# Residual GEMMs: the high weights stream high and low input as one matmul of 512 columns, and VectorE adds up two halves of a bank

## The chip, the cores and the metric

The kernel runs on one core of a Trainium2 chip. The metric is the device time of one execution in microseconds (us). A change of some 0.2% (3 us) is at the edge of what can be measured here.

## The reference

Two blocks of two layers each work on one sequence of T = 256 tokens and a width D = 1024. All matrix products are asked for in fp32:

```
block 1, layer 0: z = S5 mixer with GLU;        h = LN(a*h + z @ w_out);  h = LN(a*h + (silu(h@Wg) * (h@Wu)) @ Wdown)
block 1, layer 1: o = stick-breaking attention; h = LN(a*h + o @ w_o);    h = LN(a*h + SwiGLU(h) @ Wdown)
block 2, twice:   m = gated mix of windowed attention and mLSTM
                  x = x + m @ w_out;   u = relu(rmsnorm(x) @ w_ff1);   x = x + (u*u) @ w_ff2
```

with a = 4^(1/4). The eight products that are added to the running state (here called residual GEMMs) are the ones that the change is about: their depth is 1024 for the four w_out kinds, 2816 for the two Wdown, 4096 for the two w_ff2, and each gives 1024 x 256 results.

## The kernel before

**Split products.** Every fp32 matrix product is made of three in the type fp32r: each operand is split into a high part (a copy rounded to fp32r) and a low part (the rest), and high x high + high x low + low x high are summed in PSUM. The helper `three` (L399 to L402) issues them: `w_hi` with the input's high part, `w_hi` with its low part, `w_lo` with its high part. Each of the three is a load of 128x128 weights and a matmul of 256 columns (the tokens).

**Chunks.** Weights are streamed in chunks of 128x2048 (16 blocks of 128x128, 1 MB) through a ring of three buffers (`RING`): SyncE's DMAs bring `raw` (L371), ScalarE copies it to `w_hi` (`split_hi`, L376) once the chunk that had the buffer is used up (`chunk_done`), VectorE subtracts to get `w_lo` (`split_lo`, L381), and TensorE (PE) waits for that. The order on each engine is written out by hand, in `resid_tensor`, `resid_scalar` and `resid_vector` and their kin.

**Residual GEMMs** in the order of the program: ssm_out (0), down0 (1), sb_out (2), down1 (3), out0 (5), ff2_0 (6), out1 (7), ff2_1 (8). Their input lies in `hid_hi` and `hid_lo` (each 32 blocks of 256 tokens). The result is cut into KT = 8 tiles of 128 features x 256 tokens; a tile sums 8, 22 or 32 blocks in the first half (256 fp32) of a PSUM bank, three banks in turn (`tile_bank`). Of the ssm_out kind (shape kt8) the first chunk makes tiles 0 and 1 together, waiting for the hid blocks one by one (`resid_first`), and `resid_blocks` does the rest; of the others (shape col) `resid_blocks` does everything, tile by tile. A tile beyond the third waits until VectorE has emptied its bank (`resid_done`).

**What VectorE does with a tile.** `add_tile` (L633) adds it to `res`, scaled; before a layer norm (n < 4) tiles 4 to 7 go by `shifted_tile` (L957) to `xn`, whose mean over four tiles has been taken off ahead of time (`shift_sum` on VectorE, L939 and L941; `shift_mean` on PE, L705; `shifted_tiles`, L947 and L949). Between the tiles VectorE has the w_lo splits and, for the next GEMM, `raw_lo` or `x_lo` (L980, L998), and the sums of squares (L987, L989), while ScalarE has the w_hi splits, `raw_hi` or `x_hi` (L809, L793) and the squares (L769, L779); both take these in a fixed order. After the last tile PE makes the first chunks of the next GEMM from the not yet normed values (`early_tensor`, 258 columns) and the sums of the norm (L712 to L727), VectorE turns them into the scale (from the copy L1004 on), and ScalarE and VectorE norm four pairs of tiles in turn before they split the next weights.

Of the kernel before, what the change touches and what calls it, by code (L numbers as in the profile page):

```python
# [16 lines left out]
F32R = mybir.dt.float32r  # L17
# [3 lines left out]
ALU = mybir.AluOpType  # L21
# [3 lines left out]
P = 128  # L25
T = 256
D = 1024
KT = D // P
# [214 lines left out]
def stack(nc, w, out):  # L243
# [4 lines left out]
    with ctx:  # L248
# [14 lines left out]
        def sb(name, shape, region, off=0, dt=F32):  # L263
            return nc.alloc_sbuf_tensor_at(name, shape, dt, offset=place[region] + off)
# [5 lines left out]
        res = sb("res", [P, KT, T], "res")  # L270
        x_hi = sb("x_hi", [P, KT, T], "xh", 0, F32R)
        x_lo = sb("x_lo", [P, KT, T], "xl", 0, F32R)
        hid_hi = sb("hid_hi", [P, 32, T], "hh", 0, F32R)
        hid_lo = sb("hid_lo", [P, 32, T], "hl", 0, F32R)
        xn = sb("xn", [P, KT, T], "xc")
        sqr = sb("sqr", [P, 2, 512], "sq")
        gate_sb = sb("gate_sb", [P, RING, 512], "sg")
# [118 lines left out]
        def tile_bank(g, t):  # L396
            return OUT_BANKS[t % 3] if g.half else (g.bank0 + t) % 3

        def three(dst, lhs_hi, lhs_lo, r_hi, r_lo, start, stop):  # L399
            nc.tensor.matmul(dst, lhs_hi, r_hi, start=start, stop=False, skip_group_check=True)  # L400
            nc.tensor.matmul(dst, lhs_hi, r_lo, start=False, stop=False, skip_group_check=True)  # L401
            return nc.tensor.matmul(dst, lhs_lo, r_hi, start=False, stop=stop, skip_group_check=True)  # L402

        def weights_split(pe, chunk):
            pe.wait_ge(lo_done, chunk + 1)

# [81 lines left out]
        def resid_first(pe, g, kts=(0, KT)):  # L488

            if kts[0] == 0:  # L490
                weights_split(pe, g.c0)
                if g.half:
                    pe.wait_ge(hid_done, g.in_hid + 2)
                elif g.before.evac == "gated":
                    pe.wait_ge(z_done, g.before.gated0 + g.before.n - 1)
            s = g.c0 % RING
            hi, lo = kt8_view(w_hi, s), kt8_view(w_lo, s)
            t0 = 8 if g.half else 0
            for kt in range(*kts):
                pe.wait_ge(hid_done, g.in_hid + (kt // 2 if g.half else kt) + 1)  # L500
                for m in range(2):
                    last = three(PS[:, tile_bank(g, m), 0:T], hi[:, kt, m, :], lo[:, kt, m, :], hid_hi[:, t0 + kt, :],
                                 hid_lo[:, t0 + kt, :], kt == 0, kt == KT - 1)
                    if kt == KT - 1:
                        last.then_inc(chunk_done if m else tile_done, 1)

        def resid_blocks(pe, g, idx, j0=0, j1=16):
# [5 lines left out]
            for j in range(j0, j1):  # L513
# [11 lines left out]
                    hi, lo = kt8_view(w_hi, s)[:, kt, j // KT, :], kt8_view(w_lo, s)[:, kt, j // KT, :]  # L525
                else:
                    hi, lo = w_hi[s][:, cols], w_lo[s][:, cols]
                last = three(PS[:, tile_bank(g, t), 0:T], hi, lo, hid_hi[:, t0 + kt, :], hid_lo[:, t0 + kt, :], kt == 0,
                             kt == g.kts - 1)
                if j == 15:  # L530
                    last.then_inc(chunk_done, 1)
                elif kt == g.kts - 1:
# [96 lines left out]
        def add_tile(dve, g, t):  # L629
            tile_ready(dve, g, t)  # L630
            if t == 0 and g.normed:
                dve.wait_ge(res_normed, g.normed)
            nc.vector.scalar_tensor_tensor(out=res[:, t, :], in0=res[:, t, :], scalar=g.alpha, in1=PS[:, tile_bank(g, t), 0:T],  # L633
                                           op0=ALU.mult, op1=ALU.add).then_inc(resid_done, 1)

        def mix_bank(half, which, q):
            return (4 + half + 2 * q) if which == 0 else 2 * half + q
# [316 lines left out]
        def shifted_tile(dve, g, n, t):  # L954

            tile_ready(dve, g, t)
            nc.vector.tensor_tensor(xn[:, t, :], xn[:, t, :], PS[:, tile_bank(g, t), 0:T], ALU.add).then_inc(resid_done, 1)  # L957
            if t >= 5:
                dve.wait_ge(resid_done, g.resid0 + t + 1)

# [1728 lines left out]
```

## Time and profile before

| | |
|---|---|
| median of 3 executions | 1462.29 us (1461.01 to 1462.5) |
| the profiled execution | 1462.21 us, of which the span from first to last instruction is 1460.4 us |
| mean granted clock of TensorE | 0.98 |
| PE busy | 1383.9 us, 95%, 11695 matmuls |
| VectorE busy | 958.0 us, 66% |
| ScalarE busy | 689.7 us, 47% |
| DMA | 227.54 MB, mean 156 GB/s, queue 1 busy 54.2% of 16 engines |
| chain that ended last | PE 72%, VectorE 12%, ScalarE 9% |

PE is TensorE's matmuls, PEld its weight loads, DVE VectorE, ACT ScalarE. A matmul's duration runs from its start to its modelled end, and the next one starts before that, so a pace is read from starts. In brackets behind a row stands how long the engine had been idle before it, and who released it. Lines are those of the kernel before.

### The profile page before, as it was taken

To read this page: it belongs to the slowest core of one execution; us is meant where nothing else is said; L and a number is where in the kernel's file an instruction comes from. 1 tells how busy PE (TensorE), PEld (TensorE's weight loads), DVE (VectorE), ACT (ScalarE), POOL (GpSimd) and SP (SyncE) were. 2 spreads that over 40 slices of the span, in tenths; PEclk is the share of its full clock that TensorE was granted. 3 is DMA by queue.
4 is the path that set the end of the run, shared out by engine and by line. 5 is a ranking of instruction groups with operands and counts; after the bars stand their busy time and mean duration, and the time that the engine had idled before them with its cause. 6 is when DMAs were issued, how large, how long until landed. Compare 5 with 4: busy or idle time off the path is not lost.

```text
span 1460.4 us, 27765 instructions
## 1 busy us (share of the span) xinstructions
PE 1383.9 (95%) x11695; PEld 1342.4 (92%) x11695; DVE 958.0 (66%) x1255; ACT 689.7 (47%) x853; POOL 10.1 (1%) x8
## 2 busy tenths in 40 slices
PE   5759999999999999999989999999999999999998
PEld 4548999999988899999979998999999999899998
DVE  7996687555664587555787567765447756777542
ACT  4746463343565363343556454444344644444432
POOL 0100000000000000000000000000000000000000
PEclk7779999999999999999999999999999999999999
DMA  5078557676452457666444354557665435465761
GB/s 127 1 109 218 177 142 202 181 191 175 145 171 90 116 143 203 176 190 182 145 145 121 111 173 153 194 176 198 174 182 165 125 107 174 145 200 173 195 180 58
DMA packets 340448, 227.54 MB, mean 156 GB/s; under 512 B 21672, under 2 KB 335248, under 8 KB 340128
## 3 DMA queue, kind: packets, MB, share of 16 engines
q1 hardware_dynamic: 340352, 226.14, 54.2%
q8 instruction: 75, 1.23, 0.4%
q14 instruction: 21, 0.17, 0.0%
HBM read 222.70 MB, written 1.05 MB: 153 GB/s over the span
## 4 chain that ended last, share of the span: by engine, by line
PE 72%; DVE 12%; ACT 9%; issue 3%; SPq 2%; DMA 1%; ACTq 0%; DVEq 0%
PE PS L400 22%; PE PS L402 21%; PE PS L401 21%; DVE w_lo L381 5%; ACT w_hi L376 4%; SPq L1430 1%; PE PS L1163 1%; ACT res L815 1%; PE PS L1482 1%; DMA x_chunk<-in_x_dram 1%; PE PS L1498 1%; DVE raw_lo L980 1%; DVE sqr L987 1%; ACT x_group L1595 0%; PE PS L1463 0%
## 5 line engine op out<-in xcount | busy, mean ns | idle before, releaser
L381 DVE TENSOR_TENSOR w_lo<-raw,w_hi 128x2048 fp32r<-128x2048 f32 x208 | 475.8, 2291 | 210.0 <-ACT w_hi L376 209.9
L400 PE MATMUL PS<-x_hi,w_hi 128*128 128x256 f32 x1824 | 522.2, 286 | 8.1 <-DVE w_lo L381 7.0
L401 PE MATMUL PS<-x_lo,w_hi 128*128 128x256 f32 x1824 | 517.2, 284 | 0.0
L402 PE MATMUL PS<-x_hi,w_lo 128*128 128x256 f32 x1824 | 517.1, 283 | 0.0
L376 ACT ACTIVATE w_hi<-raw 128x2048 fp32r<-128x2048 f32 x208 | 397.1, 1910 | 230.6 <-PE PS L402 227.8
L400 PEld LDWEIGHTS PS<-x_hi,w_hi 128*128 128x128 f32 x1824 | 350.9, 192 | 12.5 <-DVE w_lo L381 8.0
L400 PE MATMUL PS<-hid_hi,w_hi 128*128 128x256 f32 x1248 | 354.5, 284 | 6.6 <-DVE hid_lo L664 6.6
L401 PE MATMUL PS<-hid_lo,w_hi 128*128 128x256 f32 x1248 | 353.1, 283 | 0.0
L402 PE MATMUL PS<-hid_hi,w_lo 128*128 128x256 f32 x1248 | 353.1, 283 | 0.0
L401 PEld LDWEIGHTS PS<-x_lo,w_hi 128*128 128x128 f32 x1824 | 351.2, 193 | 0.1
L402 PEld LDWEIGHTS PS<-x_hi,w_lo 128*128 128x128 f32 x1824 | 350.9, 192 | 0.0
L400 PEld LDWEIGHTS PS<-hid_hi,w_hi 128*128 128x128 f32 x1248 | 239.5, 192 | 7.8 <-DVE hid_lo L664 7.4
L401 PEld LDWEIGHTS PS<-hid_lo,w_hi 128*128 128x128 f32 x1248 | 239.6, 192 | 0.1
L402 PEld LDWEIGHTS PS<-hid_hi,w_lo 128*128 128x128 f32 x1248 | 239.5, 192 | 0.0
L545 ACT ACTIVATE gate_sb<-PS 128x256 f32<-128x256 f32 x48 | 18.4, 383 | 147.8 <-PE PS L402 147.8
L548 ACT ACTIVATE gate_sb<-gate_sb 128x512 f32<-128x512 f32 x32 | 20.3, 633 | 99.3 <-DVE gate_sb L601 99.3
L588 DVE TENSOR_TENSOR prod<-PS,gate_sb 128x256 f32<-128x256 f32 x48 | 20.3, 424 | 64.5 <-ACT gate_sb L545 64.4
L633 DVE SCALAR_TENSOR_TENSOR res<-res,PS 128x256 f32<-128x256 f32 x48 | 19.9, 418 | 39.2 <-PE PS L402 39.0
L400 PE MATMUL PS<-w_hi,x_hi 128*128 128x256 f32 x128 | 37.5, 293 | 0.0
L400 PE MATMUL PS<-raw_hi,w_hi 128*128 128x258 f32 x128 | 36.9, 288 | 0.0
L998 DVE SCALAR_TENSOR_TENSOR x_lo<-res,vec,x_hi 128x256 fp32r<-128x256 f32 x32 | 15.2, 484 | 33.0 <-ACT x_hi L793 33.0
L401 PE MATMUL PS<-w_lo,x_hi 128*128 128x256 f32 x128 | 36.1, 282 | 0.0
(363 smaller groups left out, 1377.3 us busy)
## 6 DMA issues: line engine op xcount, KB each, us to landing
raw<-in_w_ff_dram SPq DMA_DIRECT2D x128, 512.0 KB, 4.5
raw<-in_ffn_w_gu_dram SPq DMA_DIRECT2D x88, 512.0 KB, 5.2
raw<-in_w_in_dram SPq DMA_DIRECT2D x68, 512.0 KB, 4.8
raw<-in_sb_w_qkv_dram SPq DMA_DIRECT2D x24, 512.0 KB, 4.5
raw<-in_ffn_w_down_dram SPq DMA_DIRECT2D x20, 512.0 KB, 4.6
raw<-in_ssm_w_glu_dram SPq DMA_DIRECT2D x16, 512.0 KB, 6.4
raw<-in_w_out_dram SPq DMA_DIRECT2D x16, 512.0 KB, 4.5
raw<-in_ssm_w_out_dram SPq DMA_DIRECT2D x8, 512.0 KB, 4.5
```

Source lines behind the costliest of these rows:

```text
L376: nc.scalar.activation(w_hi[s][:, :], raw[s][:, :], ACT.Copy).then_inc(hi_done, 1)
L381: nc.vector.tensor_tensor(w_lo[s][:, :], raw[s][:, :], w_hi[s][:, :].bitcast(F32), ALU.subtract).then_inc(lo_done, 1)
L400: nc.tensor.matmul(dst, lhs_hi, r_hi, start=start, stop=False, skip_group_check=True)
L401: nc.tensor.matmul(dst, lhs_hi, r_lo, start=False, stop=False, skip_group_check=True)
L402: return nc.tensor.matmul(dst, lhs_lo, r_hi, start=False, stop=stop, skip_group_check=True)
L545: nc.scalar.activation(gate_sb[:, k, 0:T], PS[:, bank, T:2 * T], g.func).then_inc(sig_done, 1)
L548: nc.scalar.activation(gate_sb[:, k, :], gate_sb[:, k, :], ACT.Square).then_inc(u_done, 1)
L588: nc.vector.tensor_tensor(prod[:, 0:T], PS[:, bank, 0:T], gate_sb[:, k, 0:T], ALU.mult).then_inc(z_done, 1)
L633: nc.vector.scalar_tensor_tensor(out=res[:, t, :], in0=res[:, t, :], scalar=g.alpha, in1=PS[:, tile_bank(g, t), 0:T], op0=ALU.mult, op1=AL ...
L815: nc.scalar.activation(res[:, kt, :], xn[:, kt, :], ACT.Identity, scale=gain(n, kt), bias=ln_bias(n, kt)).then_inc(res_normed, 1)
L980: nc.vector.scalar_tensor_tensor(out=raw_lo[:, t, 0:T], in0=xn[:, t, :], scalar=raw_gain(n, t), in1=raw_hi[:, t, 0:T].bitcast(F32), op0=AL ...
L998: nc.vector.scalar_tensor_tensor(out=x_lo[:, t, :], in0=res[:, t, :], scalar=gain(n, t), in1=x_hi[:, t, :].bitcast(F32), op0=ALU.mult, op1 ...
```

## The change

`hid_hi` and `hid_lo` become the two halves of one tensor, `hid_both`, at the same addresses. The new helper `halves` takes the place of `three` in the residual GEMMs, for tiles 0 to 6: one matmul of `w_hi` with the high and low input as 512 columns (2 x 256, from two places 32 KB apart in each partition) into both halves of the bank, and one of `w_lo` with the high input, 256 columns, into the first half. Tile 7 keeps `three`. VectorE adds the second half of the bank to `res` or `xn` with an operation of its own: in `add_tile` after the first one, in `shifted_tile` before it, and the second of the two waits for the first (`dve_step`). The mix and all other GEMMs stay with `three`.

```diff
--- before.py
+++ after.py
@@ -270,8 +270,8 @@
         res = sb("res", [P, KT, T], "res")
         x_hi = sb("x_hi", [P, KT, T], "xh", 0, F32R)
         x_lo = sb("x_lo", [P, KT, T], "xl", 0, F32R)
-        hid_hi = sb("hid_hi", [P, 32, T], "hh", 0, F32R)
-        hid_lo = sb("hid_lo", [P, 32, T], "hl", 0, F32R)
+        hid_both = sb("hid_both", [P, 2, 32, T], "hh", 0, F32R)
+        hid_hi, hid_lo = hid_both[:, 0, :, :], hid_both[:, 1, :, :]
         xn = sb("xn", [P, KT, T], "xc")
         sqr = sb("sqr", [P, 2, 512], "sq")
         gate_sb = sb("gate_sb", [P, RING, 512], "sg")
@@ -400,6 +400,15 @@
             nc.tensor.matmul(dst, lhs_hi, r_hi, start=start, stop=False, skip_group_check=True)
             nc.tensor.matmul(dst, lhs_hi, r_lo, start=False, stop=False, skip_group_check=True)
             return nc.tensor.matmul(dst, lhs_lo, r_hi, start=False, stop=stop, skip_group_check=True)
+
+        def halves(bank, lhs_hi, lhs_lo, both, start, stop):
+
+            nc.tensor.matmul(PS[:, bank, :].rearrange("p (a t) -> p a t", a=2), lhs_hi, both, start=start, stop=False,
+                             skip_group_check=True)
+            return nc.tensor.matmul(PS[:, bank, 0:T], lhs_lo, both[:, 0, :], start=False, stop=stop, skip_group_check=True)
+
+        def in_halves(t):
+            return t < KT - 1
 
         def weights_split(pe, chunk):
             pe.wait_ge(lo_done, chunk + 1)
@@ -499,8 +508,8 @@
             for kt in range(*kts):
                 pe.wait_ge(hid_done, g.in_hid + (kt // 2 if g.half else kt) + 1)
                 for m in range(2):
-                    last = three(PS[:, tile_bank(g, m), 0:T], hi[:, kt, m, :], lo[:, kt, m, :], hid_hi[:, t0 + kt, :],
-                                 hid_lo[:, t0 + kt, :], kt == 0, kt == KT - 1)
+                    last = halves(tile_bank(g, m), hi[:, kt, m, :], lo[:, kt, m, :], hid_both[:, :, t0 + kt, :],
+                                  kt == 0, kt == KT - 1)
                     if kt == KT - 1:
                         last.then_inc(chunk_done if m else tile_done, 1)
 
@@ -525,8 +534,11 @@
                     hi, lo = kt8_view(w_hi, s)[:, kt, j // KT, :], kt8_view(w_lo, s)[:, kt, j // KT, :]
                 else:
                     hi, lo = w_hi[s][:, cols], w_lo[s][:, cols]
-                last = three(PS[:, tile_bank(g, t), 0:T], hi, lo, hid_hi[:, t0 + kt, :], hid_lo[:, t0 + kt, :], kt == 0,
-                             kt == g.kts - 1)
+                if in_halves(t):
+                    last = halves(tile_bank(g, t), hi, lo, hid_both[:, :, t0 + kt, :], kt == 0, kt == g.kts - 1)
+                else:
+                    last = three(PS[:, tile_bank(g, t), 0:T], hi, lo, hid_hi[:, t0 + kt, :], hid_lo[:, t0 + kt, :], kt == 0,
+                                 kt == g.kts - 1)
                 if j == 15:
                     last.then_inc(chunk_done, 1)
                 elif kt == g.kts - 1:
@@ -630,8 +642,15 @@
             tile_ready(dve, g, t)
             if t == 0 and g.normed:
                 dve.wait_ge(res_normed, g.normed)
-            nc.vector.scalar_tensor_tensor(out=res[:, t, :], in0=res[:, t, :], scalar=g.alpha, in1=PS[:, tile_bank(g, t), 0:T],
-                                           op0=ALU.mult, op1=ALU.add).then_inc(resid_done, 1)
+            bank = tile_bank(g, t)
+            first = nc.vector.scalar_tensor_tensor(out=res[:, t, :], in0=res[:, t, :], scalar=g.alpha, in1=PS[:, bank, 0:T],
+                                                   op0=ALU.mult, op1=ALU.add)
+            if not in_halves(t):
+                first.then_inc(resid_done, 1)
+                return
+            first.then_inc(dve_step, 1)
+            dve.wait_ge(dve_step, v_count.one())
+            nc.vector.tensor_tensor(res[:, t, :], res[:, t, :], PS[:, bank, T:2 * T], ALU.add).then_inc(resid_done, 1)
 
         def mix_bank(half, which, q):
             return (4 + half + 2 * q) if which == 0 else 2 * half + q
@@ -954,7 +973,11 @@
         def shifted_tile(dve, g, n, t):
 
             tile_ready(dve, g, t)
-            nc.vector.tensor_tensor(xn[:, t, :], xn[:, t, :], PS[:, tile_bank(g, t), 0:T], ALU.add).then_inc(resid_done, 1)
+            bank = tile_bank(g, t)
+            if in_halves(t):
+                nc.vector.tensor_tensor(xn[:, t, :], xn[:, t, :], PS[:, bank, T:2 * T], ALU.add).then_inc(dve_step, 1)
+                dve.wait_ge(dve_step, v_count.one())
+            nc.vector.tensor_tensor(xn[:, t, :], xn[:, t, :], PS[:, bank, 0:T], ALU.add).then_inc(resid_done, 1)
             if t >= 5:
                 dve.wait_ge(resid_done, g.resid0 + t + 1)
```

## Rows read from the trace of the kernel before

**Rows 1.** The page, busy us, share of the span, instructions.

```profile
PE 1383.9 (95%) x11695; PEld 1342.4 (92%) x11695; DVE 958.0 (66%) x1255; ACT 689.7 (47%) x853; POOL 10.1 (1%) x8
```

**Rows 2.** The page, costliest groups: busy, mean ns of one, idle before, releaser.

```profile
L400 PE MATMUL PS<-hid_hi,w_hi 128*128 128x256 f32 x1248 | 354.5, 284 | 6.6 <-DVE hid_lo L664 6.6
```

**Rows 3.** Windows (length, busy of each engine, clock, DMA share, GB/s), ff2 of layer 0.

```profile
995.50:1088.00 92.50, 92.50 (x773) 92.50 (x772) 46.15 (x38) 37.42 (x30) 0.00 (x0) 1.00 0.65 183
```

**Rows 4.** Timeline of PE (start, duration, us), ff2 of layer 0, first and last.

```profile
995.54 0.28 PE L400 MATMUL PS<-hid_hi,w_hi 128*128 128x256 f32 x1
...
1087.58 0.28 PE L402 MATMUL PS<-hid_hi,w_lo 128*128 128x256 f32 x1
```

**Rows 5.** Timeline of PE, 258-column matmuls without a wait, first and last of 54.

```profile
193.61 0.28 PE L401 MATMUL PS<-raw_lo,w_hi 128*128 128x258 f32 x1
...
199.95 0.28 PE L400 MATMUL PS<-raw_hi,w_hi 128*128 128x258 f32 x1
```

**Rows 6.** Windows and timeline of PE at granted clock 0.50, attention of block 2.

```profile
768.00:769.00 1.00, 1.00 (x6) 1.00 (x6) 0.50 (x3) 0.39 (x2) 0.00 (x0) 0.50 0.00 0
...
768.20 0.41 PE L400 MATMUL PS<-x_hi,w_hi 128*128 128x256 f32 x1
...
770.55 0.41 PE L402 MATMUL PS<-x_hi,w_lo 128*128 128x256 f32 x1
```

**Rows 7.** Timeline of PE, plain fp32 matmuls of the norm after ssm_out.

```profile
191.33 0.59 PE L725 MATMUL PS<-xn,const 128*128 128x256 f32 x2
...
193.06 0.59 PE L718 MATMUL PS<-sqr,const 128*128 128x256 f32 x2
```

**Rows 8.** Timeline of PE's weight loads behind the plain fp32 matmul in down0.

```profile
354.35 0.19 PEld L400 LDWEIGHTS PS<-hid_hi,w_hi 128*128 128x128 f32 x1
354.56 0.19 PEld L401 LDWEIGHTS PS<-hid_lo,w_hi 128*128 128x128 f32 x1
354.68 0.19 PEld L402 LDWEIGHTS PS<-hid_hi,w_lo 128*128 128x128 f32 x1
```

**Rows 9.** Timeline of PE, plain fp32 matmuls of 129 columns.

```profile
813.21 0.39 PE L2059 MATMUL PS<-vm_tok,m_w 128*128 128x129 f32 x2
813.43 0.39 PE L2060 MATMUL PS<-vm_tok,m_w 128*128 128x129 f32 x2
```

**Rows 10.** Timeline of VectorE, two operations of which one waits for the other.

```profile
194.62 0.42 DVE L1004 COPY dm_sb<-PS 128x256 f32<-128x256 f32 x1
195.07 0.42 DVE L1006 TENSOR_TENSOR rstd<-dm_sb,PS 128x256 f32<-128x256 f32 x1
```

**Rows 11.** Windows and timeline, the norm after ssm_out: VectorE's stretch, its start, PE's wait.

```profile
178.20:194.60 16.40, 16.40 (x128) 16.04 (x127) 16.07 (x23) 9.36 (x15) 0.00 (x0) 1.00 0.38 102
...
176.28 1.92 ACT L376 ACTIVATE w_hi<-raw 128x2048 fp32r<-128x2048 f32 x1 [2.22 <-PE PS L402]
...
209.66 0.39 PE L400 MATMUL PS<-x_hi,w_hi 128*128 128x256 f32 x1 [1.66 <-DVE w_lo L381]
```

**Rows 12.** Timeline, down0 and its norm: waits of PE, the chain's start and copy.

```profile
354.03 0.30 PEld L705 LDWEIGHTS PS<-prod,const 128*128 128x128 f32 x2 [0.29 <-DVE prod L941]
...
366.27 1.91 ACT L376 ACTIVATE w_hi<-raw 128x2048 fp32r<-128x2048 f32 x1 [1.20 <-PE PS L402]
...
389.41 0.42 DVE L1004 COPY dm_sb<-PS 128x256 f32<-128x256 f32 x1
...
404.23 0.39 PE L400 MATMUL PS<-x_hi,w_hi 128*128 128x256 f32 x1 [0.90 <-DVE w_lo L381]
```

**Rows 13.** Timeline, out0: PE behind the mix, tile 7's x_lo, PE behind the squares.

```profile
882.83 0.38 PE L400 MATMUL PS<-hid_hi,w_hi 128*128 128x256 f32 x1 [1.61 <-DVE hid_lo L664]
...
905.54 0.48 DVE L998 SCALAR_TENSOR_TENSOR x_lo<-res,vec,x_hi 128x256 fp32r<-128x256 f32 x1 [0.58 <-ACT x_hi L793]
...
908.19 0.70 PE L714 MATMUL PS<-sqr,const 128*128 128x256 f32 x2 [0.19 <-ACT sqr L779]
```

## The prediction

> **What bounds the kernel now.** I read the page's busy times first: TensorE is busy 95% of the span [rows 1], so the question is what its matmuls are paced by. The costliest groups show the operation that the change touches: 1248 triples on hid [rows 2], of which 128 belong to the mix GEMMs and 1120 to the residual ones (4 x 64 + 2 x 176 + 2 x 256). The windows show a long residual stage, ff2 of layer 0: PE is busy for all of it, VectorE for half, at clock 1.00 [rows 3]. The timeline gives the pace, which the mean duration of 283 ns hides because matmuls overlap: from the first to the last start of that stage are 767 steps in 92.04 us, 120.0 ns a step [rows 4]. Then I read, in the timelines of VectorE and ScalarE, the places where PE does wait: the layer norms at the end of ssm_out, down0, sb_out and down1, and the end of out0 and out1.
>
> **What a step of 120 ns consists of.** Four rows bound it. The 258-column matmuls take 53 steps in 6.34 us, 119.6 ns, no more than 256 columns do [rows 5]: neither a rate per column nor a fixed cost on top of the columns sets the 120 ns, or 258 would be slower by almost 1 ns. At granted clock 0.50 (1.2 GHz) the same fp32r matmuls take 11 steps in 2.35 us, 213.6 ns, which is 256/1.2 = 213.3 with nothing beside it [rows 6]. At full clock the plain fp32 matmuls of the norm, which also load 128x128, take 1.73 us for eight (four lines, x2 each), 216 ns [rows 7]. The weight loads behind such a matmul start at 354.35, 354.56 and 354.68: 0.21 after the long one, 0.12 after the short one, each load with the start of the matmul before its own [rows 8]. So I read: a load of fp32r weights starts when the matmul ahead starts and takes 120 ns; a matmul with less than that to stream waits for it, one of 213 ns hides it.
>
> **The pair in place of the triple.** One triple: 3 x 120 = 360 ns. New: 512 columns (512/2.4 = 213.3; 216 by rows 7) with the low load hidden, then 256 columns under which the next high load takes its 120: 336 ns. It saves 24 ns. Bounds: the most is 360 - 213 - 110 = 37 ns, if the short one went at the 110 ns that plain fp32 loads show (0.22 us for two) [rows 9]; the least is 360 - 512 x 0.464 - 120 = 2.5 ns, if 119.6/258 = 0.464 ns were a rate per column [rows 5]. I take 24, since rows 6 to 8 agree on it. Pairs: 980 (all residual triples but those of tile 7: 1120 - 140). 980 x 24 ns = 23.5 us off PE's own work. How much of it arrives is a matter of each stage.
>
> The Trainium skill (TensorE: Matmul & The Clock Gate, section Back-to-back issue gap) gives N/2.4 + 2.5 ns for a warm matmul, 109 ns at 256 columns. The trace disagrees with 120.0 [rows 4]. By that rule a pair would save one fixed 2.5 ns, 2.5 us in all: it speaks against this change, and its time is that of rival 2.
>
> **What VectorE pays.** Seven tiles of eight get a second add, behind a wait for the first one. A dependent 128x256 operation follows its forerunner after 0.45 us [rows 10]. 56 x 0.45 = 25 us more on VectorE, which has room in the ff2 stages [rows 3] and none in the norm tails. Its wait stands on VectorE's own semaphore, so everything behind it there slips by 0.45: the split into w_lo, raw_lo, the sums.
>
> *ff2_0 and ff2_1.* 224 pairs each, no wait of PE inside. Their last tile keeps the triple, so the end has one add as now. The loads stay hidden: a chunk goes from 5.76 to 5.38 us, DMA share 0.65 to 0.70 [rows 3], and ScalarE's 1.9 plus VectorE's 2.3 us a chunk are still under it. 2 x 224 x 24 ns = -10.8 us.
>
> *ssm_out and sb_out.* In the 16.4 us before the norm VectorE is busy 16.07, with no gap [rows 11]. The stretch begins when chunk 1 is done (ScalarE's w_hi at 176.28, VectorE's w_lo at 178.23) [rows 11] and ends with the copy at 194.62 [rows 10]; the norm's result lets PE go on at 209.66, after a wait of 1.66 [rows 11]. In ssm_out chunk 1 comes 32 x 24 ns = 0.77 earlier, but tile 3's second add (0.45) eats most of it: w_lo starts 0.45 earlier. Tiles 4, 5 and 6 add 3 x 0.45 = 1.35. Net +0.9. In sb_out the pairs before PE's wait for the last heads gain nothing, 24 remain (0.58), w_lo starts 0.27 earlier: net +1.1. The PE time saved there becomes a longer wait.
>
> *down0 and down1.* PE already waits 0.29 at the shift's matmul for VectorE's sum (the load at 354.03) [rows 12]. That sum comes from chunk 4 (80 pairs, -1.92) plus tile 3's 0.45, so at -1.47, though PE is there at -2.30: 0.83 is lost. Two chunks later (32 pairs, 0.77) chunk 7 is done at -2.24, and from there ScalarE's w_hi at 366.27 starts a chain through VectorE and ScalarE, in turn, to the copy at 389.41 and to PE's restart at 404.23 [rows 12]. It has the second adds of tiles 5 and 6, +0.90. Net -1.34 each, -2.7 for both.
>
> *out0 and out1.* The first block waits for VectorE's mix until 882.83 [rows 13], so 44 pairs remain, 1.06 us. But each tile goes ScalarE's x_hi, VectorE's x_lo, next add in turn. Tile 1's second add is absorbed by idle time ahead of tile 2's x_hi; those of tiles 3 and 4 (0.9) use up the idle time there and the 0.9 by which chunk 2 comes earlier, with +0.1 left at tile 4's x_hi; those of 5 and 6 come on top: +1.0 at tile 7's x_lo, now 905.54 [rows 13]. PE is early by 1.06 and waits for it. The squares follow, and there PE already waits 0.19 [rows 13]. Net +1.0 each, +2.0.
>
> Sum: -10.8 - 2.7 + 0.9 + 1.1 + 2.0 = -9.5. The profiled execution took 1462.2 us (span 1460.4 and 1.8 around it), the median is 1462.29; so **1452.7 us**.
>
> **Rivals.**
> (1) *VectorE's adds cost nothing on the path, and the PE time arrives whole*: -23.5, 1438.7 us. For it: PE at 95%. Against it: rows 11 to 13, where PE waits for that chain at the end of six stages. Chance 0.08.
> (2) *The change makes it slower because the 512 columns stream at a rate per column.* Place: the long matmul; price: 238 ns instead of 216. A pair then saves 2.5 ns, ff2 gives -1.1 in all, the downs about +1.0 each, ssm_out and sb_out +1.35 each, out0 and out1 +1.4 each: +6.4, 1468.6 us. It decides from a saving of some 10 ns a pair downward. The same holds if the input from two regions 32 KB apart is streamed as two pieces with the load repeated: the change then wouldn't do what it says. Against it: 258 columns take no longer than 256 [rows 5]. Chance 0.06. (The rule of the Trainium skill above would give a pair the same 2.5 ns.)
> (3) *The 13 ns over 106.7 are a fixed cost per matmul.* A pair saves 13.3 ns: ff2 -6.0, the downs -0.1 each, ssm_out and sb_out +1.3 each, out0 and out1 +1.2 each: -1.2, 1461.0 us. For it: 120 - 106.7 = 13.3 is there in every step. Against it: 216 rather than 227 [rows 7], and rows 5. Chance 0.12.
> The forecast's mechanism holds the remaining 0.74.
>
> **How the numbers follow.** The likeliest case gives 1452.7. Its own range is 1446 to 1459: a pair at 37 ns gives 1444 to 1446, and 15 ns with 0.6 us an add gives some 1460. The range to hold 8 of 10 is 1445 to 1461: it takes in most of case 3 and leaves out 1 and 2. A difference of 0.2% (2.9 us) is about what a measurement of this kernel can tell. Faster than 1459.4: the forecast, case 1 and little of case 3, 0.83. Within: most of case 3, 0.10. Slower: case 2 and a misjudged VectorE, 0.07.
>
> **What would show it.** 980 matmuls fewer. In ff2 the start of a long matmul to the next short one 0.21 to 0.22 (case 3: 0.227, case 2: 0.238), from there 0.12; the stage in 86.7 instead of 92.0 us. The copy of the norm later than now, counted from chunk 1, in ssm_out and sb_out, and PE's waits there at about 3.9 us in place of 1.66 (56 x 24 ns = 1.3 earlier, 0.9 later). At the shift of down0 a wait of 1.1 us. In out0, tile 7's x_lo later against the end of the mix by 1.0. The forecast is wrong if the short matmul doesn't keep to 120, if the second add follows after other than 0.45, or if the tails of the norms move with PE.

## The result: 0.4% slower, and the profile after

| | before | after |
|---|---|---|
| median, executions | 1462.50 us, 7 | 1468.77 us, 7 |
| ratio, 95% interval | | 1.0039, 1.0026 to 1.0051 |
| profiled execution, its span | 1462.2, 1460.4 | 1467.8, 1466.0 |

The forecast was 1452.7 us, 1445 to 1461. By the interval the change made the kernel slower by 3.8 to 7.5 us. One of the seven executions after took 1522 us, at a mean granted clock of 0.845 where the others have 0.974 to 0.991, and is not in the ratio.

The page of the kernel after, in the order of [rows 1, 2] (the lines of the file have shifted: L406 is the matmul of 512 columns, L408 the one of 256 behind it):

```profile
PE 1384.1 (94%) x10715; PEld 1294.0 (88%) x10715; DVE 979.3 (67%) x1311; ACT 689.6 (47%) x853; POOL 10.1 (1%) x8
...
L406 PE MATMUL PS<-hid_both,w_hi 128*128 128x512 f32 x980 | 348.3, 400 | 6.7 <-DVE hid_both L683 6.7
...
L408 PE MATMUL PS<-hid_both,w_lo 128*128 128x256 f32 x980 | 275.6, 281 | 0.0
```

There are 980 matmuls fewer (11695 - 10715) and 56 VectorE operations more, as counted; PE's busy time has not moved (1383.9 to 1384.1). The window over ff2 of layer 0 [rows 3] and PE's timeline in it, first, a few in the middle, last [rows 4]:

```profile
1004.45:1095.00 90.55, 90.55 (x546) 80.13 (x545) 48.89 (x44) 37.37 (x29) 0.00 (x0) 1.00 0.67 186
...
1004.45 0.40 PE L406 MATMUL PS<-hid_both,w_hi 128*128 128x512 f32 x1
...
1010.10 0.40 PE L406 MATMUL PS<-hid_both,w_hi 128*128 128x512 f32 x1
1010.34 0.28 PE L408 MATMUL PS<-hid_both,w_lo 128*128 128x256 f32 x1
1010.46 0.40 PE L406 MATMUL PS<-hid_both,w_hi 128*128 128x512 f32 x1
1010.69 0.28 PE L408 MATMUL PS<-hid_both,w_lo 128*128 128x256 f32 x1
...
1094.99 0.28 PE L402 MATMUL PS<-hid_both,w_lo 128*128 128x256 f32 x1
```

The stage takes 90.54 us from start to start, 1.50 less than before, where 5.4 was forecast. Tile 7's triples are 95 steps of 0.12 (11.4 us); the 224 pairs share the other 79.14: **353.3 ns a pair, 6.7 less than a triple**. From long to short are some 0.235, from short to long 0.118.

The ends of the other stages, [rows 11 to 13] after the change. PE's timeline first, then ScalarE and VectorE in the norm behind ssm_out (w_hi, w_lo, copy), in the one behind down0 (w_hi, copy) and at the end of out0 (tile 7's x_lo, PE behind the squares):

```profile
210.21 0.39 PE L400 MATMUL PS<-x_hi,w_hi 128*128 128x256 f32 x1 [1.76 <-DVE w_lo L381]
355.97 0.70 PE L724 MATMUL PS<-prod,const 128*128 128x256 f32 x2 [0.66 <-DVE prod L960]
406.85 0.39 PE L400 MATMUL PS<-x_hi,w_hi 128*128 128x256 f32 x1 [1.76 <-DVE w_lo L381]
543.17 0.39 PE L400 MATMUL PS<-x_hi,w_hi 128*128 128x256 f32 x1 [1.77 <-DVE w_lo L381]
739.09 0.39 PE L400 MATMUL PS<-x_hi,w_hi 128*128 128x256 f32 x1 [2.43 <-DVE w_lo L381]
...
175.29 1.92 ACT L376 ACTIVATE w_hi<-raw 128x2048 fp32r<-128x2048 f32 x1 [2.12 <-PE PS L408]
177.44 2.28 DVE L381 TENSOR_TENSOR w_lo<-raw,w_hi 128x2048 fp32r<-128x2048 f32 x1
195.19 0.42 DVE L1027 COPY dm_sb<-PS 128x256 f32<-128x256 f32 x1
...
368.00 1.93 ACT L376 ACTIVATE w_hi<-raw 128x2048 fp32r<-128x2048 f32 x1 [1.09 <-PE PS L408]
...
392.05 0.42 DVE L1027 COPY dm_sb<-PS 128x256 f32<-128x256 f32 x1
...
914.45 0.48 DVE L1021 SCALAR_TENSOR_TENSOR x_lo<-res,vec,x_hi 128x256 fp32r<-128x256 f32 x1 [0.58 <-ACT x_hi L812]
...
917.09 0.70 PE L733 MATMUL PS<-sqr,const 128*128 128x256 f32 x2 [0.22 <-ACT sqr L798]
```

Every wait at a norm has grown, those that end at 210.21 and 543.17 by 0.1 us only (before: 1.66, 0.90, 1.65 and 1.64 for the four in order; after: 1.76, 1.76, 1.77 and 2.43). Measured from the first matmul of a residual GEMM to PE's restart behind the norm (for out0 and out1 from the mix's end to the last squares), the stages moved so:

| us | ssm_out | down0 | sb_out | down1 | out0 | ff2_0 | out1 | ff2_1 | sum |
|---|---|---|---|---|---|---|---|---|---|
| before | 45.10 | 85.01 | 47.26 | 85.75 | 25.36 | 92.04 | 25.37 | 92.04 | |
| after | 46.43 | 85.62 | 48.66 | 86.36 | 26.54 | 90.54 | 26.55 | 90.55 | |
| moved | +1.33 | +0.61 | +1.40 | +0.61 | +1.18 | -1.50 | +1.18 | -1.49 | **+3.3** |

The medians moved by 6.3 and the ratio says 5.7, so 2.4 to 3 us are not in the stages. The windows show what else differs: two places right behind waits at a norm, in the kernel after and then at the same times before (length, busy time of each engine, clock, DMA share, GB/s).

```profile
210.00:215.00 5.00, 4.79 (x27) 4.79 (x28) 4.93 (x8) 0.51 (x1) 0.00 (x0) 0.66 0.74 199
740.00:743.00 3.00, 3.00 (x16) 3.00 (x15) 2.93 (x5) 0.63 (x1) 0.00 (x0) 0.50 0.94 288
```

```profile
210.00:215.00 5.00, 5.00 (x44) 5.00 (x43) 4.93 (x8) 0.65 (x2) 0.00 (x0) 1.00 0.86 228
740.00:743.00 3.00, 2.90 (x27) 1.81 (x26) 1.75 (x5) 2.46 (x8) 0.00 (x0) 1.00 0.75 237
```

After the waits that end at 210.21 and 739.09, PE runs 15 steps each at clock 0.50, every one 213 ns in place of 120. I call such a step slow; it costs 0.093 us. Past the first 125 us, PE's timeline has 27 slow steps before and 65 after: +3.5 us in this pair of profiles, of which 30 steps (2.8 us) stand behind those two waits; the other 35, and the 27 of before, lie in the attention of block 2 (765 to 830 and 1184 to 1190). With the stages' +3.3, and the stretch ahead of ssm_out, which happened to be 0.8 shorter (163.78 in place of 164.56), that makes 6.0 us; the two spans differ by 5.6.

### The profile page after: what moved, and what is told of

It reads as the page before. It is cut to its first block, busy times and chain, and to the rows that moved or that the text cites. A ratio compares the mean times of both kernels' runs of the same rounds, so it can differ in the third digit from the quotient of the medians.

```text
span 1466.0 us, 25861 instructions
## 1 busy us (share of the span) xinstructions
PE 1384.1 (94%) x10715; PEld 1294.0 (88%) x10715; DVE 979.3 (67%) x1311; ACT 689.6 (47%) x853; POOL 10.1 (1%) x8
## 4 chain that ended last, share of the span: by engine, by line
PE 70%; DVE 14%; ACT 9%; issue 3%; SPq 2%; DMA 1%; ACTq 0%; DVEq 0%
PE PS L400 15%; PE PS L401 15%; PE PS L402 15%; PE PS L406 12%; PE PS L408 6%; DVE w_lo L381 5%; ACT w_hi L376 4%; SPq L1453 1%; PE PS L1186 1%; DMA x_chunk<-in_x_dram 1%; PE PS L1505 1%; ACT x_hi L812 1%; ACT res L834 1%; DVE raw_lo L1003 1%; PE PS L1521 1%
## 5 line engine op out<-in xcount | busy, mean ns | idle before, releaser
L406 PE MATMUL PS<-hid_both,w_hi 128*128 128x512 f32 x980 | 348.3, 400 | 6.7 <-DVE hid_both L683 6.7
L402 PEld LDWEIGHTS PS<-x_hi,w_lo 128*128 128x128 f32 x1824 | 353.3, 194 | 0.0
L408 PE MATMUL PS<-hid_both,w_lo 128*128 128x256 f32 x980 | 275.6, 281 | 0.0
L406 PEld LDWEIGHTS PS<-hid_both,w_hi 128*128 128x128 f32 x980 | 184.4, 188 | 53.2 <-DVE hid_both L683 8.0
L408 PEld LDWEIGHTS PS<-hid_both,w_lo 128*128 128x128 f32 x980 | 185.6, 189 | 0.1
L402 PE MATMUL PS<-hid_both,w_lo 128*128 128x256 f32 x268 | 76.0, 284 | 0.0
L401 PE MATMUL PS<-hid_both,w_hi 128*128 128x256 f32 x268 | 76.0, 284 | 0.0
L400 PE MATMUL PS<-hid_both,w_hi 128*128 128x256 f32 x268 | 76.0, 283 | 0.0
L400 PEld LDWEIGHTS PS<-hid_both,w_hi 128*128 128x128 f32 x268 | 51.5, 192 | 0.4
L402 PEld LDWEIGHTS PS<-hid_both,w_lo 128*128 128x128 f32 x268 | 51.5, 192 | 0.0
L401 PEld LDWEIGHTS PS<-hid_both,w_hi 128*128 128x128 f32 x268 | 51.5, 192 | 0.0
```

Of the source, the lines that this page charges most:

```text
L406: nc.tensor.matmul(PS[:, bank, :].rearrange("p (a t) -> p a t", a=2), lhs_hi, both, start=start, stop=False, skip_group_check=True)
L408: return nc.tensor.matmul(PS[:, bank, 0:T], lhs_lo, both[:, 0, :], start=False, stop=stop, skip_group_check=True)
```

## Experiments

My theory after the comparison had three terms: a pair saves 6.7 ns and not 24 (why, was open); the second adds lengthen the ends of six stages as the prediction's account of VectorE has it; PE's longer waits bring on stretches at half clock. Twelve runs were made, of eleven kernels. "Before" was timed beside each set, at 1462.4 to 1463.5 us.

**1. Matmuls by themselves** (`bench`; it leaves the whole of the reference's computation out). Series of 48 matmuls on each other's heels, every one with a load of its own:

```
for i in range(48): mm(PS[:, 0, 0:N], w(i), x[:, 256 * (i % 24):256 * (i % 24) + N])    # N = 128, 192, 256, ... 512
for i in range(48): mm(PS[:, 1, :] as 2 x 256, w(i), both[:, :, i % 32, :])             # 512 from two regions
for i in range(24): mm(512 columns, w(2 * i)); mm(256 columns, w(2 * i + 1))             # the pairs
```

> Computes nothing of the reference: it only times series of 48 back-to-back matmuls, each with its own load of 128x128 weights, with ScalarE and VectorE idle and then (last three series) with both at work on SBUF. Question: why does the 512-column fp32r matmul take 235 ns from its start to the next (pair 353.3 ns) and not 214 to 216. Theory R (a rate per column of fp32r at full clock): pace = N x 0.459 ns wherever that is more than the time of a load; so 512 columns 235, 448 about 206, 384 about 177, 320 about 148, and the same for contiguous columns as for two regions; 128 and 192 columns at the pace of the load alone, somewhere at 107 to 118. bf16 at 512 then 216. Theory A (address): two regions 32 KB apart cost it; contiguous 512 columns 216, two regions 235. Theory C (contention): 216 in the quiet series and 235 in those beside ScalarE and VectorE. Theory F (fixed cost of about 13 to 22 ns per matmul): 128 columns at 67 to 75, 384 at 173 to 182.

PE's timeline of that kernel, the first row of each series (L63 has 128 columns, L65 192, L67 256, L69 320, L71 384, L73 448, L75 512, L77 512 from two regions, L79 512 over eight banks, L81 and L82 the pairs in one region, L84 in two, then L87):

```profile
32.80 0.56 PE L63 MATMUL PS<-both,wts 128*128 128x128 f32 x4
38.11 0.53 PE L65 MATMUL PS<-both,wts 128*128 128x192 f32 x3
43.50 0.54 PE L67 MATMUL PS<-both,wts 128*128 128x256 f32 x3
49.27 0.60 PE L69 MATMUL PS<-both,wts 128*128 128x320 f32 x3
56.31 0.51 PE L71 MATMUL PS<-both,wts 128*128 128x384 f32 x2
64.64 0.57 PE L73 MATMUL PS<-both,wts 128*128 128x448 f32 x2
74.55 0.63 PE L75 MATMUL PS<-both,wts 128*128 128x512 f32 x2
85.48 0.61 PE L77 MATMUL PS<-both,wts 128*128 128x512 f32 x2
96.36 0.62 PE L79 MATMUL PS<-both,wts 128*128 128x512 f32 x2
107.24 0.39 PE L81 MATMUL PS<-both,wts 128*128 128x512 f32 x1
107.47 0.28 PE L82 MATMUL PS<-both,wts 128*128 128x256 f32 x1
107.58 0.40 PE L81 MATMUL PS<-both,wts 128*128 128x512 f32 x1
...
115.71 0.40 PE L84 MATMUL PS<-both,wts 128*128 128x512 f32 x1
...
124.19 0.50 PE L87 MATMUL PS<-bx,bw 128*128 128x256 bf16 x3
```

From series start to series start, by 48: 110.6 ns at 128 columns, 112.3 at 192, 120.2 at 256, 146.7 at 320, 173.5 at 384, 206.5 at 448, 227.7 at 512, 226.7 from two regions and over the banks. With N/2.4 taken off, 13.5 are left at 256, 13.3 at 320, 13.5 at 384, and 13.3 at 512 (14.4 in the contiguous series): **at the two lengths of the pair, some 13.3 ns on each fp32r matmul at full clock beside its columns**, over a floor of some 110. It is not one constant for every length: at 448 columns 19.8 are left (and by experiment 2's kernel 11.7 at 288 and 16.6 at 480). I read the floor, and not the 120, as what a load of weights takes; at 256 columns it is hidden already. This rules out the reading of the prediction (load of 120, free streaming), under which 512 columns take 216, and rival 2's rate per column (235 to 238 there), and address or bank as causes: two regions cost nothing. By these paces a pair should take 346.7; it takes 8.47 us / 24 = 352.9 in one region and 353.3 in two. So 6.6 ns a pair are lost to something else, alone as in the kernel.

**2. The order of long and short** (`bench2`, again nothing of the reference): the same 24 + 24 matmuls alternating, in groups of two long and two short, of four, of eight.

> Computes nothing of the reference: series of back-to-back fp32r matmuls as before. The first bench gave 120.2 ns at 256 columns, 146.7 at 320, 226.7 at 512 in a row of equals (a fixed 13.3 ns beside columns/2.4), contiguous or from two regions, quiet or beside ScalarE and VectorE; and 353 for 512 and 256 in alternation, 6.6 more than the sum of the two. Theory S (each change of the column count costs some 3.3 ns): 353.3 a pair in alternation, 350.0 in groups of two, 348.3 in groups of four, 347.5 in groups of eight. Theory P (the pair costs 353.3 in any order): 353.3 throughout. For 258 columns: 120.8 by the fixed cost, 119.6 if the odd length counts otherwise, as the norm's rows had it.

PE's timeline, first rows of series: 256 columns (L71), then two at a time (L77, L79), four (L82, L84), eight (L87, L89), 258 columns (L91). The alternating series runs from 50.44 to 58.92.

```profile
44.68 0.52 PE L71 MATMUL PS<-both,wts 128*128 128x256 f32 x3
...
58.92 0.63 PE L77 MATMUL PS<-both,wts 128*128 128x512 f32 x2
...
67.28 0.63 PE L82 MATMUL PS<-both,wts 128*128 128x512 f32 x2
...
75.70 0.63 PE L87 MATMUL PS<-both,wts 128*128 128x512 f32 x2
...
84.08 0.52 PE L91 MATMUL PS<-both,wts 128*128 128x258 f32 x3
```

A pair takes 353.3 ns alternating, 348.3 in groups of two, 350.8 in fours, 349.2 in eights. So the extra depends on the order (theory P is out), but not as theory S has it, by the number of changes: groups of two do best, and larger ones do worse again. The single starts in the trace show where it lies. In the groups of eight the long matmuls take 233, 236, 228, 233 and 230 ns before they settle at 227, and the short ones 114 and 119 before they settle at 120; alternating, the long ones stay at 233 to 241 and the short ones at 113 to 120. The cost sits in the first long ones behind a change of length. What in the chip makes it, these runs don't show. 258 columns take 120.6 here, and 256 at the same stride 119.0: with that scatter the comparison that [rows 5] were used for can't tell 0.8 ns.

**3 and 4. One half of the change each.** `ff2_only` has pairs in the two ff2 stages, where VectorE has room; `tails_only` in the other six GEMMs.

```diff
-        def in_halves(t):
-            return t < KT - 1
+        def in_halves(g, t):
+            return g.kts == 32 and t < KT - 1        # ff2_only;  tails_only: g.kts != 32
```

> Pairs and second adds in ff2_0 and ff2_1 alone (448 pairs), the triple in the six other residual GEMMs. Theory now (a pair saves 6.7 ns, what is added on VectorE costs only in the norm tails): 448 x 6.7 = 3.0 us off, 1459.5 where before is 1462.5, ratio 0.998, each ff2 stage 90.5 instead of 92.0 us. Rival (VectorE's adds cost in ff2 too, or the lost clock follows the change anywhere): 1462 or more.

> The complement: pairs and second adds in ssm_out, sb_out, down0, down1, out0 and out1 (532 pairs), the triple in both ff2. Theory now: the adds lengthen the chain before the norms by more than the pairs take off PE: +1.3, +1.4, +0.6, +0.6, +1.2, +1.2 = +6.3 us, and 0 to 3 us more for stretches at half clock behind PE's longer waits: 1469 to 1472 where before is 1462.5. Rival (the loss of the change lies in the matmuls themselves, or in chance of the clock): 1461 to 1464.

`tails_only`: 1472.0 us, ratio 1.0065 (1.0052 to 1.0077), at the upper end of what was expected. Its stages sum to +5.8; the 6 GEMMs with a norm or squares behind them are where the loss is. `ff2_only`: 1462.3, ratio 0.9996 (0.9987 to 1.0006); the 3 us that its stages save (90.55 and 90.54 from start to start) did not show. Its profile has 48 slow steps against 27. Experiment 9 comes back to it.

**5. The adds without the pairs** (`adds_only`): the 512 columns are two matmuls of 256 into the two halves of the bank, so PE does the old work and VectorE the new.

```diff
-            nc.tensor.matmul(PS[:, bank, :].rearrange("p (a t) -> p a t", a=2), lhs_hi, both, start=start, stop=False,
-                             skip_group_check=True)
+            nc.tensor.matmul(PS[:, bank, 0:T], lhs_hi, both[:, 0, :], start=start, stop=False, skip_group_check=True)
+            nc.tensor.matmul(PS[:, bank, T:2 * T], lhs_hi, both[:, 1, :], start=False, stop=False, skip_group_check=True)
```

> The second adds without the 512-column matmul: w_hi with the high input goes to the first half of the bank and w_hi with the low input to the second, as two matmuls of 256 columns, everywhere where the change has its pair. PE's work is that of before. Theory now: all of VectorE's cost and no gain: ssm_out and sb_out +1.6 each, down0 and down1 +1.3 each, out0 and out1 +1.4 each, ff2 0, so +8.6, and 0 to 3 for the clock: 1471 to 1474 where before is 1462.5. Rival (the second adds are hidden and the 512-column matmuls cost time): 1462 to 1464.

1476.7 us, ratio 1.0089 (1.0075 to 1.0104): more than expected. Its stages sum to +8.2 (ssm_out +1.54, down0 +1.34, sb_out +1.55, down1 +1.34, out0 and out1 +1.2 each, ff2 0.0). So the adds cost 8.2, the pairs give back 4.9 in all (3.0 of it in ff2), and the change's +3.3 is the difference. The rest, 4.8 us by the ratio, has, in the profile, half-clock stretches of 15 steps behind three of its four restarts, 409.06, 545.70 and 743.82 (4.2 us); the window behind the first:

```profile
410.00:413.50 3.50, 3.50 (x19) 3.50 (x18) 3.46 (x6) 0.75 (x2) 0.00 (x0) 0.51 0.96 322
```

**6 and 7. The waits filled** (`after_busy`, `before_busy`): both kernels with dummy matmuls that write a free bank, 12 before each norm's restart (16 behind down1), 20 in each attention of block 2.

```diff
+        def keep_busy(n, bank):
+            for i in range(n):
+                nc.tensor.matmul(PS[:, bank, 0:T], x_hi[:, 0, 0:P], x_hi[:, 1, :], start=True, stop=True,
+                                 skip_group_check=True)
...
+                if begins and head and idx == 3 and g.func is ACT.Silu:
+                    keep_busy(12, bank_of(g, k))
```

> The changed kernel with dummy matmuls on PE (results overwritten) just ahead of four waits behind the norms and of one in each attention of block 2 (12 to 20 of 120 ns, 1.4 to 2.4 us, less than or about the wait that they fill). Theory K (behind its longer waits PE runs at half clock for 3.4 us at a time, which is where 2 to 3 us of the loss come from): the mean clock goes from 0.978 to 0.985 and more, the time to 1464.5 to 1466.5 where the change is 1468.8. Rival (the clock falls by chance elsewhere): 1468 to 1470.

> The kernel before with the same dummy matmuls. Theory K: little to gain, since its waits are shorter, 27 slow steps of 93 ns at most (2.5 us): 1460 to 1462.5. Rival (dummies only delay what comes after): 1463 to 1466.

They came out at 1468.6 and 1466.3 us, both above what theory K expected and where the rivals had them. The dummies cost before 3 to 4 us by themselves, most of it in the second attention (1089.55 to 1253.35, 163.8 us, in place of 1087.58 to 1248.98, 161.4), so neither says what the clock is worth in the whole. What they do say: the restart of down1's norm in `after_busy`, and the windows behind two restarts that ran at 0.50 or 0.66 without dummies, are

```profile
737.18 0.39 PE L400 MATMUL PS<-x_hi,w_hi 128*128 128x256 f32 x1 [0.51 <-DVE w_lo L381]
...
210.00:215.00 5.00, 5.00 (x42) 5.00 (x43) 4.93 (x7) 0.51 (x1) 0.00 (x0) 1.00 0.78 215
738.00:743.00 5.00, 5.00 (x44) 5.00 (x43) 4.86 (x8) 1.36 (x4) 0.00 (x0) 1.00 0.98 313
```

and between the two kernels the change is worth +2.3 us by the medians, +3.5 by the ratios (1.0046 against 1.0022). That is the stages' 3.3 with nothing left over, but the two intervals together leave some 1 to 6 us, which takes in the 5.7 of the kernels without dummies too: it agrees with the theory and doesn't prove it.

**8 and 10. Pairs where the second add is covered** (`early_busy` with the dummies, `early_too` without): ff2 as in the change, ahead of a norm tiles 0 to 2 alone, none in out0 and out1.

```diff
+        def in_halves(g, t):
+            return t < (KT - 1 if g.kts == 32 else 0 if g.half else 3)
```

> Pairs in both ff2 (tiles 0 to 6) and in ssm_out, sb_out, down0 and down1 for tiles 0 to 2 alone, none in out0 and out1, so that no second add lies on a chain before a norm; with the dummy matmuls. Theory now: -3.0 from ff2, about -0.4 each from down0 and down1, -0.2 each from ssm_out and sb_out, 0 to -2.5 by the clock: 1456 to 1458.5. Rival (tile 0 to 2's adds do reach the chain, or the clock falls all the same): 1460 or more.

> Pairs in ff2 (tiles 0 to 6) and, of the residual GEMMs ahead of a layer norm, in tiles 0 to 2 only (their second adds lie ahead of the stretch in which VectorE has no gap); none in out0 and out1; no dummy matmuls. The same edit stood between two kernels with dummies: 1466.3 without it, 1461.7 with it, so -4.6 us. Theory A (what a pair saves, 6.7 ns, and the place of the second adds account for the time, and the clock's half-speed stretches lie as before): 1462.4 - 4.6 = 1457.8 us, each ff2 stage 90.5 us, waits ahead of the first attention's GEMM of ssm_out within 0.2 us of before. Rival K (any edit that moves PE's waits brings new half-clock stretches; with ff2 alone they took back all of 3.0 us): 1460.5 to 1462.5, with more than 40 slow steps past 120 us where before has 27.

`early_busy` 1461.7 against `before_busy` 1466.3, -4.6, but above the 1456 to 1458.5 expected and in the rival's range, since the dummies cost 3 to 4 us. `early_too` **1458.4 us, ratio 0.9966 (0.9954 to 0.9978)**, as theory A has it. The stages: ssm_out -0.17, down0 -0.45, sb_out -0.09, down1 -0.45, ff2 -3.0, together -4.2. PE's restart behind down1's norm has its old wait back (1.61; 1.64 before, 2.43 after the change):

```profile
734.49 0.39 PE L400 MATMUL PS<-x_hi,w_hi 128*128 128x256 f32 x1 [1.61 <-DVE w_lo L381]
```

Rival K, by which any moved wait brings on half clock, fails here on both of its signs, the time and the slow steps (18, where it asked for over 40). A profile's count of slow steps says little by itself, though: the same kernel has 48 and 19 in experiments 4 and 9, and the two kernels of experiments 11 and 12 have 46 and 44, all of them in the attention of block 2.

**9. `ff2_only` again,** on another chip, since its loss was the one result that fitted nothing.

> The kernel with pairs in the two ff2 stages alone, a second time and on another chip: the first time its stages were 3.0 us shorter in all but its median stood only 0.2 us under before. Open is whether that loss belongs to the kernel (some wait that it moves always brings on more half-clock stretches) or to that set of executions. If to the kernel: a ratio of 0.999 to 1.000 again. If to the set: about 0.998 (3.0 us under before).

1462.3 us, ratio 0.9992 (0.9983 to 1.0002): between the two, and with the first time a loss of some 2 us that seems to belong to the kernel. Its profile has 19 slow steps, fewer than before, and the stages' -3.0. The difference lies behind the last matmul of ff2. From its start to the end of the span are 8.7 us (8.4 the first time), and 6.7 in all other kernels. The output's four DMAs are issued as always, but their median landing is later; the DMA view (operation, count, KB each, us to landing) of this kernel, and of before:

```profile
out_dram<-out_sb SPq DMA_DIRECT2D x4, 256.0 KB, 2.8
```

```profile
out_dram<-out_sb SPq DMA_DIRECT2D x4, 256.0 KB, 2.4
```

The queues show what else moves there. DMA rate from 1450 to 1465 us in 40 slices, before and then `ff2_only`, with the queue that `ff2_only` alone has in it (packets, MB, share):

```profile
GB/s 0 0 0 0 0 0 0 0 0 0 0 0 0 0 0 0 0 0 317 393 366 377 399 366 388 191 0 0 0 0 0 0 0 0 0 0 0 0 0 0
...
GB/s 0 0 0 0 0 0 0 0 0 0 0 0 0 0 0 0 251 388 399 371 355 361 377 230 27 22 27 27 5 0 0 0 0 0 0 0 0 0 0 0
q8 instruction: 1, 0.02, 0.6%
```

In both profiles of this kernel one packet of the instruction queue, 16 KB and some 1.4 us long, starts while the output is being written (at 1456.91 and 1453.33), and the output then ends in a trickle. In the profiles of the kernels with a normal end the last such packet starts 6 us and more ahead of the first output DMA. In `ff2_grouped` (experiment 12) it starts at 1458.42, behind the span, which ends at 1456.60; there 2.9 us of the execution lie outside the span, in place of 1.8. So the fetching of instructions, which falls elsewhere in each kernel, is the likely cause. That is read from its place alone: no run moved the packet. Nor is it the same in every execution: 1.7 to 1.9 us lie outside the span throughout in the other kernels, 2.0 to 3.3 in some executions of these two.

**11 and 12. The order of experiment 2 in the kernel:** `early_grouped` is `early_too`, `ff2_grouped` is `ff2_only`, with two long matmuls, then their two short ones, in ff2.

```diff
+                if in_halves(g, t) and g.kts == 32:
+                    both, bank = hid_both[:, :, t0 + kt, :], tile_bank(g, t)
+                    long_part(bank, hi, both, kt == 0)
+                    if kt % 2 == 0:
+                        put_off = (lo, both)
+                        continue
+                    short_part(bank, *put_off, False)
+                    last = short_part(bank, lo, both, kt == g.kts - 1)
```

> early_too, with the matmuls of the ff2 pairs in groups of two: two of 512 columns, then two of 256. In the series by itself such a group took 348.3 ns a pair against 353.3 alternating. Theory G (the 5 ns per pair carry over): each ff2 stage 1.1 us shorter than in early_too (90.5 to 89.4), median 2.2 us less than early_too, about 1455.6. Rival (the extra comes from the weight loads' alternation only in a bare series, or the waits on w_lo at chunk starts hide it): 90.5 and no difference. With rival K on top the median may be up to 3 us off in either case, so the stage time decides.

> Pairs in the two ff2 stages alone, issued in groups of two long and two short matmuls. Stage sum: 2 x (92.04 - 89.42) = 5.2 us under before, 2.3 under the alternating order. If the stage sum is all there is: ratio 0.9964. If ff2 alone always loses some 3 us to the clock: 0.9985. Against the kernel with pairs in tiles 0 to 2 ahead of the norms too (0.9945) it tells what those are worth: by the stage sums 1.2 us.

`early_grouped` **1456.4 us, ratio 0.9945 (0.9932 to 0.9959), the fastest kernel of this case** (1455.6 was expected); `ff2_grouped` 1459.1, 0.9965 (0.9950 to 0.9980), where the stage sum alone gives 0.9964. PE's timeline in the first, the stage's first row, some of the middle, its last:

```profile
996.04 0.63 PE L405 MATMUL PS<-hid_both,w_hi 128*128 128x512 f32 x2
...
1009.97 0.63 PE L405 MATMUL PS<-hid_both,w_hi 128*128 128x512 f32 x2
1010.44 0.39 PE L409 MATMUL PS<-hid_both,w_lo 128*128 128x256 f32 x2
1010.67 0.63 PE L405 MATMUL PS<-hid_both,w_hi 128*128 128x512 f32 x2
...
1085.46 0.28 PE L402 MATMUL PS<-hid_both,w_lo 128*128 128x256 f32 x1
```

The stage takes 89.42 us in both, 1.12 less than alternating, which is 224 x 5.0 ns: the series' number to the last digit.

**All of it on one sheet.** "Stages" is the sum over the eight stages in the trace, "output" what the span's end behind the last matmul took longer in the profile, "measured" (ratio - 1) x 1462.4:

| us | stages | output | measured (95%) | rest |
|---|---|---|---|---|
| after | +3.3 | 0 | +5.7 (3.8 to 7.5) | +2.4 |
| tails_only | +5.8 | 0 | +9.5 (7.6 to 11.3) | +3.7 |
| adds_only | +8.2 | 0 | +13.0 (11.0 to 15.2) | +4.8 |
| ff2_only, ff2_again | -3.0 | +1.8, +2.0 | -0.6, -1.2 (-2.5 to +0.9) | +0.6, -0.2 |
| ff2_grouped | -5.2 | 0 | -5.1 (-7.3 to -2.9) | +0.1 |
| early_too | -4.2 | 0 | -5.0 (-6.7 to -3.2) | -0.8 |
| early_grouped | -6.4 | 0 | -8.0 (-9.9 to -6.0) | -1.6 |

The three kernels that lengthen PE's waits at the norms have a rest of 2.4 to 4.8 us, and their intervals leave out the stages' sum; the other five runs have none that the measurement can tell. The profiles of the three, and of none of the others, have half-clock stretches right behind those restarts: of their 12 waits (1.75 to 2.43 us) six were followed by 15 slow steps, two in after, one in `tails_only` and three in `adds_only`; of the 24 waits of 0.88 to 1.66 us in before and the other five runs, none. Two a profile at 1.4 us are 2.8 us, an estimate that fits the rests.

Profile by profile the account closes. The sum of stages, output, slow steps and the stretch ahead of ssm_out against the difference of the spans is 6.0 against 5.6 in after, 7.1 against 7.1 in `tails_only`, 16.5 against 16.2 in `adds_only`, -3.8 against -3.8 in `early_too`, -3.0 against -3.3 in `early_grouped`, -3.7 against -3.8 in `ff2_grouped` and -2.5 against -2.6 in `ff2_again`; the one that misses is `ff2_only`, +0.3 against +1.0.

For the medians the third term stays likely and not shown. A profile is one execution, and in that of after the waits at 406.85 and 543.17 were followed by full clock. A wait of 1.76 against one of 1.66 is a small difference to hang it on. And the mean granted clock of an execution doesn't order the times: the fastest of after had 0.991 (1466.95 us), and those of before with the same 0.991 took 1460.7 to 1464.0, as those with less did. That figure decides nothing either way.

## Why the prediction was wrong

**What a step of 120 ns consists of, and the pair's 24 ns: the step that failed.** It said that a load takes 120 and hides behind a long matmul, so that 512 columns cost 216. Measured: 226.7 for the long one, 10.7 more, and 6.6 more for alternating; of the 24 ns, 6.7 are left. In the sum, ff2's -10.8 became -3.0, and the savings in the other six shrank by the same factor, so that these went from +1.3 to +6.3: together the -9.5 became the stages' +3.3. The rows misled in one way each. [Rows 6] show no cost beside the columns, but at half clock, where the bench's 13.3 ns aren't seen; [rows 7] show none, but for plain fp32 (the series confirm 216 a pass); [rows 5] can't resolve it. None of them was fp32r, at full clock, and longer than the load: that row wasn't in the trace, and the bound from 2.5 to 37 should have been kept wide open instead of being closed by three rows of other kinds.

The Trainium skill (TensorE: Matmul & The Clock Gate, Back-to-back issue gap) has a fixed part of 2.5 ns on N/2.4. For bf16 the series of experiment 1 agree with it, 109.4 ns at 256 columns and 215.8 at 512; for fp32r the part beside the columns is 13.3 at these two lengths, and 11.7 to 19.8 at others. By that page a pair gives 2.5, against 6.7 measured.

**What VectorE pays: right, to 0.2 us a stage.** With 6.7 put for 24, the prediction's account reads: ssm_out, tiles 4 to 6 at 1.35 and w_lo no earlier (177.44, at the same distance from the first matmul as before), the copy 1.36 later against w_lo; measured +1.33. down0: from w_hi to the copy 24.05 us in place of 23.14 [rows 12], +0.91 where +0.90 was said, and w_hi only 0.28 earlier where 2.24 was said; measured +0.61. out0: x_lo of tile 7 at 23.90 behind the mix in place of 22.71 [rows 13], +1.2; rival 3 had +1.2. Sum of the six, +6.3.

**Rival 3 (fixed 13.3 ns, 1461.0)** had the right cause at the two lengths used and too large a saving, since nothing in its account speaks of alternation. **Rival 2's 1468.6** met the time by luck, with numbers that were wrong: 512 columns at no rate per column, and a saving of 2.5. It did have the point from which the sign turns (some 10 ns a pair), and the measured 6.7 lies below it; and its +6.4 is stages alone, where the stages measured +3.3. Its chance of 0.06, beside 0.12, was far too small for two readings that no row excluded.

**A term that was missing:** 2.4 to 3 of the 5.7 to 6.3 us stand outside the stages, where the prediction had nothing. The clock is the likely place: the prediction let PE's waits grow at the norms and gave them no price but their length. Without this term the sum would still have been off by 12.8.

**The signs.** 980 fewer matmuls, yes. Long to short 0.235, over the 0.227 of rival 3. The shift's wait in down0: 0.66, forecast 1.1. PE before the norms' GEMMs: 1.76 and not 3.9, since PE didn't come so early.

## What to carry to other kernels

Joining two matmuls whose loads are hidden saves what they cost beside their columns: 13.3 ns here for two fp32r matmuls of 256 columns made into one of 512. Half of that is lost when long and short ones alternate; grouped by twos, 5.0 of the 6.6 ns came back. An operation put on the engine that feeds the norms costs its full 0.45 us each time once that engine has no gap. In this kernel the change paid in the stages with room and ahead of the gapless stretch (-8 us with both and the grouping), and lost 6 when made everywhere. Where the price of an operation isn't in the trace in the same type, clock and size, the range has to stay as wide as its bounds.

## What the runs showed of the hardware

- fp32r at full clock: beside N/2.4, 13.3 to 13.5 ns at 256, 320, 384 and 512 columns, but 11.7 at 288, 19.8 at 448 and 16.6 at 480; a floor of 110.6 ns at 128; no such part at half clock (213.6 at 256 [rows 6]).
- 512 columns read from two regions 32 KB apart cost nothing (226.7 against 227.7).
- A pair of 512 and 256 columns: 353.3 ns alternating, 348.3 by twos, 350.8 by fours, 349.2 by eights; behind a change of length the first five long ones take 228 to 236 in place of 227.
- Behind a wait of PE of 1.75 to 2.43 us the granted clock fell to 0.50 for 15 steps, at a cost of 1.4 us, in six of 12 cases; behind waits of 0.88 to 1.66 us in none of 24.
- One packet of 16 KB on the instruction queue, 1.4 us long, fell into the writing of the output in both profiles of one kernel, on two chips, and the span's end came 1.8 to 2.0 us later; that the packet is the cause is likely and untested.
